# Alternating the transposes of cached keys and of probabilities in a fused decoder layer's attention

## The chip, the cores and the metric

One core of a Trainium2 chip runs the whole program. Its engines work side by side, each through its own list of instructions, and meet at semaphores: TensorE (PE: matmuls and transposes, results to the eight PSUM banks), VectorE (DVE), ScalarE (ACT), GpSimd (POOL), and SyncE (SP), which issues the DMAs. The metric is device microseconds of one execution, lower is better.

## The reference, cut to what matters

One layer step for a prompt of 1024 tokens and for 8 samples of 8 new tokens. The change lies in the first attention of both.

```python
for window, dil in ((128, 1), (512, 4), (2048, 16)):     # 12 heads of 64
    # prompt: every query over strided keys of the prompt
    # sample: 8 queries over strided keys of a cache of 2048 rows and the 8 new rows
    s = einsum(q, k) * 64 ** -0.5 + bias(distance)
    p, lse = softmax(s), logsumexp(s)
    out = p @ v
att = combine(outs, lses)                                # by the softmax denominators
x = x + concat(att, conv) @ w_out                        # then cross attention, SwiGLU, final norm
```

The three branches are folded into one softmax over all keys, by a bias row that holds the branches' weights and masks.

## The kernel before

The attention stage has 24 **steps** `d` for the prompt (6 pairs of heads by 4 pairs of query blocks) and 12 **units** `u` for the samples (two samples, four heads each). Two steps go with one unit: `d = 2u` is the even step, `d = 2u + 1` the odd one. TensorE's list for a step (lines 1207 to 1226) is what the change touches.

- `turn_p(d - 1)`: the probabilities of the step before (tile `sp`, 18 blocks of 128x128) are transposed, four blocks to a PSUM bank, with two blocks of spread reciprocals (`rrec`) behind them. It fills five banks. ScalarE copies each to `p_T` (L1667).
- `turn_keys(u, j)`: cached keys (tile `kb`, loaded by DMA) are transposed, four blocks to a bank. An even step does `j = 0` (four banks) right after `turn_p`, and `j = 1` (four banks) later. An odd step does `j = 2` (two banks). VectorE copies each to `kt01` or `kt2` (L2117).
- `turn_sample_p(u - 1)`, in even steps: the samples' probabilities of the unit before (`srow`) are transposed, three banks. They must have gone through ScalarE's exponential `sample_softmax` (L1678, semaphore `sx_done`).
- `scores(d)`: six matmuls q by k to banks 0 to 3. VectorE adds the bias and takes the maximum (L2126), ScalarE takes the exponential (L1673).
- `sample_scores`, `sample_values`, `values(d - 1)`: the rest of the step's products (L1126, L1131, L1196, L1172).

All transposes and values share the three banks 4, 5 and 6. The table `FILL` numbers the fills of these banks in TensorE's order. Fill `f` goes to bank `4 + f % 3`, and TensorE waits before it (`t_free`) until the fill three before it has been copied out. The copying engines read the same table, so they follow any order of it.

ScalarE's list for an even step (L1690 on) is: the five copies of `turned_p(d - 1)`, then `sample_softmax(u - 1)`, then `turned_sample_p(u - 1)`, then `softmax(d)`. VectorE's is: in every eighth step first `new_rows` (L2110, 16 small copies of bias rows), the key copies, the bias and maximum of the scores, and so on. The diff changes neither list but for the banks named in it.

SyncE reloads a key buffer when its last bank has been transposed (`keys_turned`, L714). There are two buffers, so `j = 2` of one unit and `j = 1` of the next share one.

Of the kernel before, what the change touches and what calls it, by code (L numbers as in the profile page):

```python
# [26 lines left out]
P = 128  # L27
# [54 lines left out]
def layer_step(nc, A):  # L82

    ctx = ExitStack()
    with ctx:
        def sem(name):
            return ctx.enter_context(nc.semaphore(name))
# [257 lines left out]
        kn_in = [sem(f"kn_in{i}") for i in range(2)]  # L345
# [142 lines left out]
        FILL = {}  # L488

        def number(kind, at, count):  # L490
            for i in range(count):
                FILL[kind, at, i] = len(FILL)

        for d in range(STEPS):
            u, second = divmod(d, 2)
            if d:
                number("P", d - 1, 5)
            if second:
                number("K2", u, 2)
                if u:  # L500
                    number("OS", u - 1, 1)
                number("O", d - 1, 1)
                if u:
                    number("OT", u - 1, 1)
            else:
                number("K0", u, 4)
                if u:
                    number("PS", u - 1, 3)
                number("K1", u, 4)
                if d:  # L510
                    number("O", d - 1, 1)
# [6 lines left out]
        KEY_DMAS = (6, 6, 2)  # L518
# [6 lines left out]
        def member_columns(g):  # L525
            return slice(P * (g // 2), P * (g // 2) + P)
# [39 lines left out]
        def _(sp_):  # L566
# [248 lines left out]
            def part_done(kind, n, i=0):  # L815
                _, b, turn = xfill(kind, n, i)
                sp_.wait_ge(xf_full[b], turn + 1)
# [155 lines left out]
        def _(pe):  # L973
# [116 lines left out]
            def fill(kind, at, i=0):  # L1090

                f = FILL[kind, at, i]
                if f >= 3:
                    pe.wait_ge(t_free[f % 3], f // 3)
                return bank[4 + f % 3], t_full[f % 3]
# [4 lines left out]
                    f = FILL[kind, at, i]  # L1100
                    pe.wait_ge(t_free[f % 3], f // 3 + 1)

            def turn_keys(u, j):

                q = 3 * u + j
                turns = q // 2 + 1
                pe.wait_ge(kn_in[q % 2], 16 * sum(KEY_DMAS[p % 3] for p in range(q % 2, q + 1, 2)))
                for i in range(2 if j == 2 else 4):
                    out, full = fill(f"K{j}", u, i)
                    for k in range(4):  # L1110
                        g, t = (i, k) if j < 2 else (2 * i + k // 2, k % 2)
                        last = pe.transpose(out[:, k * P:(k + 1) * P], kb[q % 2][:, g % 2, t, member_columns(g)],  # L1112
                                            ident[:, :])
                    last.then_inc(full, 1)

            def sample_scores(u, j):

                emptied(f"K{j}", u, 2 if j == 2 else 4)
                if 3 * u + j:
                    pe.wait_ge(sr_done, 3 * u + j)  # L1120
                else:
                    pe.wait_ge(kv_done, 36)
                for g in range(4):
                    c, b = member(u, g)
                    keys = kt2[:, g, :] if j == 2 else kt01[:, g, :]
                    last = pe.matmul(bank[7][32 * g:32 * g + 32, 0:256 if j == 2 else 512], q_blk[:, c, b, :], keys,  # L1126
                                     start=True, stop=True)
                if j == 2:
                    for g in (0, 2):
                        c, b = member(u, g)  # L1130
                        last = pe.matmul(bank[7][32 * g:32 * g + 64, 256:256 + TS],  # L1131
                                         q_blk[:, c, b:b + 2, :].rearrange("p b r -> p (b r)"),
                                         k_T[c][:, TP:T], start=True, stop=True)
                last.then_inc(st_ready, 1)

            def scores(d):

                c = d // 4
                for m, (h, _, _, n, key0, qb, at) in enumerate(chunks(d)):
                    if m >= 4:  # L1140
                        pe.wait_ge(sc_free, 6 * d + m - 3)
                    elif d:
                        pe.wait_ge(sc_free, 6 * (d - 1) + (m + 5 if m < 2 else m + 1))
                    half = slice(HD * h, HD * h + HD)
                    pe.matmul(bank[at][:, 0:n], q_T[c][half, qb * P:(qb + 1) * P], k_T[c][half, key0:key0 + n],
                              start=True, stop=True).then_inc(sc_ready, 1)

            def turn_p(d):

                for i in range(5):  # L1150
                    pe.wait_ge(ex_done, 4 * d + (3 if i < 2 else 4))
                    out, full = fill("P", d, i)
                    for k in range(4 * i, min(18, 4 * i + 4)):
                        h, at = divmod(k, 9)
                        last = pe.transpose(out[:, (k - 4 * i) * P:(k - 4 * i + 1) * P], sp[:, h, at * P:(at + 1) * P],
                                            ident[:, :])
                    if i == 4:
                        pe.wait_ge(rr_spread, 4 * d + 4)
                        for s in range(2):
                            last = pe.transpose(out[:, (2 + s) * P:(3 + s) * P], rrec[:, s, :], ident[:, :])  # L1160
                    last.then_inc(full, 1)

            def values(d):

                c, a = divmod(d, 4)
                emptied("P", d, 5)
                out, full = fill("O", d)
                for s, qb in enumerate((a, 7 - a)):
                    for k in range(qb + 1):
                        for h in range(2):  # L1170
                            at = 9 * h + (a + 1) * s + k
                            last = pe.matmul(out[HD * h:HD * h + HD, s * P:(s + 1) * P],  # L1172
                                             v_nat[c][:, k, HD * h:HD * h + HD], p_T[:, at * P:(at + 1) * P],
                                             start=k == 0, stop=k == qb)
                last.then_inc(full, 1)

            def turn_sample_p(u):

                pe.wait_ge(sx_done, u + 1)
                for i, (t0, t1) in enumerate(NEW_TILES):  # L1180
                    out, full = fill("PS", u, i)
                    for t in range(t0, t1):
                        n = P if t < KT else TS
                        last = pe.transpose(out[0:n, (t - t0) * P:(t - t0 + 1) * P], srow[:, t * P:t * P + n], ident[:, :])
                    last.then_inc(full, 1)

            def sample_values(u):

                emptied("PS", u, 3)
                pe.wait_ge(vn_in, 16 * VALUE_DMAS * (u + 1))  # L1190
                out, full = fill("OS", u)
                for t in range(KT + 1):
                    for g in range(4):
                        c = member(u, g)[0]
                        keys = vn[:, g % 2, t, member_columns(g)] if t < KT else vs_nat[:, c * P:(c + 1) * P]
                        last = pe.matmul(out[32 * g:32 * g + 32, 0:P], pT_s[:, t, 32 * g:32 * g + 32], keys,  # L1196
                                         start=t == 0, stop=t == KT)
                last.then_inc(full, 1)

            def turn_sample_out(u):  # L1200
                emptied("OS", u, 1)
                out, full = fill("OT", u)
                pe.transpose(out[:, 0:P], o_sb[:, :], ident[:, :]).then_inc(full, 1)
# [2 lines left out]
            pe.wait_ge(kv_done, 6 * PAIRS)  # L1206
            for d in range(STEPS):
                u, second = divmod(d, 2)
                if d:
                    turn_p(d - 1)  # L1210
                turn_keys(u, 2 if second else 0)
                if u and not second:
                    turn_sample_p(u - 1)
                scores(d)
                if second:
                    sample_scores(u, 1)
                    if u:
                        sample_values(u - 1)
                    sample_scores(u, 2)
                else:  # L1220
                    sample_scores(u, 0)
                    turn_keys(u, 1)
                if d:
                    values(d - 1)
                if second and u:
                    turn_sample_out(u - 1)
# [230 lines left out]
            for v in range(XU + 3):  # L1457
# [8 lines left out]
                if 2 <= v < XU + 2:  # L1466
                    u = v - 2
# [7 lines left out]
                if v >= 3 and (v - 3) % 4 == 3:  # L1475
                    u = v - 3
# [1126 lines left out]
```

## Time and profile before

| | |
|---|---|
| median of 3 runs | 2029.76 us (2029.33 to 2029.76) |
| profiled execution | 2030.58 us |
| its span in the trace | 2028.8 us |
| TensorE busy over the span | 94% |
| granted TensorE clock, mean | 0.983 |
| attention stage (first to last key transposes) | 327.9 to 657.0 us |

Times in the rows are us from the span's start. "Idle before" is the time that an engine waited ahead of a group of instructions, and after the arrow stands what ended the wait. Matmuls overlap each other, so a group's first start and the next group's first start tell more than the durations.

### The profile page before, as it was taken

How to read it: one execution, taken by the hardware profiler on the slowest of the kernel's cores; microseconds unless marked ns; L12 is line 12 of the kernel's file. 1: busy time of each engine (PE TensorE's matmuls, PEld its weight loads, DVE VectorE, ACT ScalarE, POOL GpSimd, SP SyncE). 2: the span in 40 equal slices, each digit the busy share in tenths (PEclk: the TensorE clock that was granted, in tenths of full speed). 3: DMA queues.
4: the chain of work that ended last, by engine and by line, in shares of the span. 5: the costliest groups of instructions: out<-in, count | busy, mean ns of one | idle time of the engine just before them, and what ended most of it. 6: DMA issues, size and time to landing. Idle time of an engine off the chain costs nothing. (4 is left out here: it accounts for less than half of the span.)

```text
span 2028.8 us, 33274 instructions
## 1 busy us (share of the span) xinstructions
PE 1906.5 (94%) x13253; PEld 1764.3 (87%) x13253; DVE 1049.0 (52%) x2108; ACT 440.4 (22%) x902; POOL 508.5 (25%) x377
## 2 busy tenths in 40 slices
PE   6999996999999899899989999999999999999987
PEld 6999995666666799899648989999999999999987
DVE  6698635676666453512543354544544544544455
ACT  5000022555455421200431131001001001000005
POOL 2333221010100134452002223233332233333220
PEclk9999998999999999999999989999999999999998
DMA  4499958698888612124530123432433342311102
GB/s 150 141 339 339 311 177 205 158 212 212 212 208 220 182 42 73 52 84 147 175 105 21 47 70 132 166 124 83 165 124 113 144 161 86 124 42 47 46 21 89
DMA packets 221891, 281.38 MB, mean 139 GB/s; under 512 B 9409, under 2 KB 208457, under 8 KB 220041
## 3 DMA queue, kind: packets, MB, share of 16 engines
q1 hardware_dynamic: 221789, 279.95, 45.5%
q8 instruction: 72, 1.18, 0.2%
q14 instruction: 30, 0.25, 0.0%
HBM read 266.48 MB, written 113.89 MB: 187 GB/s over the span
## 5 line engine op out<-in xcount | busy, mean ns | idle before, releaser
L908 POOL CAST w_hi<-w_raw 128x1024 fp32r<-128x1024 f32 x98 | 105.3, 1075 | 980.2 <-issue 332.8
L1526 PE MATMUL bank<-g_lo,w_hi 128*128 128x362 f32 (+1 forms) x1056 | 350.4, 332 | 0.0
L1526 PE MATMUL bank<-g_hi,w_lo 128*128 128x362 f32 (+1 forms) x1056 | 350.3, 332 | 0.0
L1526 PE MATMUL bank<-g_hi,w_hi 128*128 128x362 f32 (+1 forms) x1056 | 347.8, 329 | 2.2 <-DVE g_lo L2454 2.2
L910 POOL TENSOR_TENSOR w_lo<-w_raw,w_hi 128x1024 fp32r<-128x1024 f32 x98 | 265.3, 2707 | 7.8
L1526 PEld LDWEIGHTS bank<-g_hi,w_hi 128*128 128x128 f32 x1056 | 199.7, 189 | 2.6 <-DVE g_lo L2454 2.5
L1526 PEld LDWEIGHTS bank<-g_hi,w_lo 128*128 128x128 f32 x1056 | 201.0, 190 | 0.0
L2531 DVE TENSOR_TENSOR xT<-bank,xT 128x362 f32<-128x362 f32 (+1 forms) x264 | 139.8, 534 | 116.2 <-PE bank L1546 116.2
L1526 PEld LDWEIGHTS bank<-g_lo,w_hi 128*128 128x128 f32 x1056 | 199.5, 189 | 0.0
L1546 PE MATMUL bank<-act_hi,w_hi 128*128 128x364 f32 (+1 forms) x528 | 176.3, 334 | 16.3 <-DVE xT L2531 10.2
L1546 PE MATMUL bank<-act_lo,w_hi 128*128 128x364 f32 (+1 forms) x528 | 174.2, 330 | 0.0
L1546 PE MATMUL bank<-act_hi,w_lo 128*128 128x364 f32 (+1 forms) x528 | 174.2, 330 | 0.0
L1054 PE MATMUL bank<-h_hi,w_hi 128*128 128x362 f32 (+1 forms) x432 | 146.1, 338 | 5.3 <-POOL w_lo L910 5.3
L1054 PE MATMUL bank<-h_hi,w_lo 128*128 128x362 f32 (+1 forms) x432 | 142.5, 330 | 0.0
L1054 PE MATMUL bank<-h_lo,w_hi 128*128 128x362 f32 (+1 forms) x432 | 142.3, 329 | 0.0
L1289 PE MATMUL bank<-g_hi,w_hi 128*128 128x362 f32 (+1 forms) x384 | 127.7, 333 | 3.5 <-DVE g_lo L2225 2.8
L1289 PE MATMUL bank<-g_lo,w_hi 128*128 128x362 f32 (+1 forms) x384 | 129.8, 338 | 0.0
L1289 PE MATMUL bank<-g_hi,w_lo 128*128 128x362 f32 (+1 forms) x384 | 127.5, 332 | 0.0
L1546 PEld LDWEIGHTS bank<-act_hi,w_hi 128*128 128x128 f32 x528 | 100.2, 190 | 21.4 <-DVE xT L2531 15.1
L2482 DVE TENSOR_TENSOR f_in<-bank,factor 128x362 f32<-128x362 f32 (+1 forms) x66 | 35.1, 534 | 145.9 <-PE bank L1526 145.7
L2487 DVE SCALAR_TENSOR_TENSOR gated<-gated,bank 128x362 f32<-128x362 f32 (+1 forms) x66 | 34.9, 528 | 143.2 <-PE bank L1526 143.2
L2117 DVE COPY kt<-bank 128x512 f32<-128x512 f32 x120 | 75.4, 683 | 64.6 <-PE bank L1112 64.5
(289 smaller groups left out, 3651.3 us busy)
## 6 DMA issues: line engine op xcount, KB each, us to landing
out_sk_dram<-in_cache_win_k_dram SPq DMA_DIRECT2D x24, 2040.0 KB
out_sv_dram<-in_cache_win_v_dram SPq DMA_DIRECT2D x24, 2040.0 KB
vn<-in_cache_win_v_dram SPq DMA_DIRECT2D x24, 576.0 KB, 7.4
kb<-in_cache_win_k_dram SPq DMA_DIRECT2D x48, 256.0 KB, 5.4
vn<-in_cache_win_v_dram SPq DMA_DIRECT2D x24, 512.0 KB, 8.9
w_raw<-in_w_in_dram SPq DMA_DIRECT2D x22, 512.0 KB, 10.2
w_raw<-in_w_ffn_gate_dram SPq DMA_DIRECT2D x22, 512.0 KB, 3.8
w_raw<-in_w_ffn_up_dram SPq DMA_DIRECT2D x22, 512.0 KB, 3.8
```

The costliest lines, as they stand in the source:

```text
L908: pool.tensor_copy(w_hi[slot][:, :], w_raw[slot][:, :]).then_inc(w_hi_done, 1)
L910: pool.tensor_tensor(w_lo[slot][:, :], w_raw[slot][:, :], w_hi[slot][:, :].bitcast(F32), ALU.subtract).then_inc(w_ready[slot], 1)
L1054: last = pe.matmul(out, w, r, start=start, stop=stop)
L1289: last = pe.matmul(out, w, r, start=start, stop=stop)
L1526: last = pe.matmul(out, w, r, start=start, stop=stop)
L1546: last = pe.matmul(bank[6 + r % 2][:, 0:w], wt[slot][:, j * 512 + o * P:j * 512 + (o + 1) * P], rhs[:, j, t0:t0 + w], start=j == 0 and m == 0,
L2117: dve.tensor_copy(dst, src[:, :]).then_inc(free, 1)
L2482: dve.tensor_tensor(f_in[:, t0:t0 + w], bank[g][:, 0:w], factor[:, t0:t0 + w], ALU.mult).then_inc(f_gate, 1)
L2487: dve.scalar_tensor_tensor(out=out, in0=out, scalar=0.5, in1=bank[3 + g][:, 0:w], op0=ALU.mult, op1=ALU.mult).then_inc(f_gated, 1)
L2531: dve.tensor_tensor(place, bank[6 + r % 2][:, 0:w], place, ALU.add).then_inc(d_added, 1)
```

## The change

In a step, TensorE now goes through the fills P0, key 0, P1, key 1 and so on, until the keys of that place (four banks in an even step, two in an odd one) run out, and then through the rest of P. `FILL` is numbered so too. The wait for the keys' DMA stands before the first key fill, which is now the second fill of the step and was the sixth.

```diff
+        def first_keys(d):
+            return ("K2", 2) if d % 2 else ("K0", 4)
+
         for d in range(STEPS):
             u, second = divmod(d, 2)
-            if d:
-                number("P", d - 1, 5)
+            kind, count = first_keys(d)
+            for i in range(5):
+                if d:
+                    FILL["P", d - 1, i] = len(FILL)
+                if i < count:
+                    FILL[kind, u, i] = len(FILL)
             if second:
-                number("K2", u, 2)
...
             else:
-                number("K0", u, 4)
...
-            def turn_keys(u, j):
+            def turn_keys(u, j, fills):
                 q = 3 * u + j
-                turns = q // 2 + 1
-                pe.wait_ge(kn_in[q % 2], 16 * sum(KEY_DMAS[p % 3] for p in range(q % 2, q + 1, 2)))
-                for i in range(2 if j == 2 else 4):
+                if 0 in fills:
+                    pe.wait_ge(kn_in[q % 2], 16 * sum(KEY_DMAS[p % 3] for p in range(q % 2, q + 1, 2)))
+                for i in fills:
...
-            def turn_p(d):
-                for i in range(5):
+            def turn_p(d, fills=range(5)):
+                for i in fills:
...
             for d in range(STEPS):
                 u, second = divmod(d, 2)
-                if d:
-                    turn_p(d - 1)
-                turn_keys(u, 2 if second else 0)
+                for i in range(5):
+                    if d:
+                        turn_p(d - 1, [i])
+                    if i < first_keys(d)[1]:
+                        turn_keys(u, 2 if second else 0, [i])
                 if u and not second:
                     turn_sample_p(u - 1)
                 scores(d)
...
-                    turn_keys(u, 1)
+                    turn_keys(u, 1, range(4))
```

TensorE in even step 6, before: `sp` and `rrec` are the probabilities with their reciprocals, `kb1` the keys, `srow` the samples' probabilities.

```order
L1155 MATMUL bank5<-ident,sp 128x128 x4
L1155 MATMUL bank6<-ident,sp 128x128 x4
L1155 MATMUL bank4<-ident,sp 128x128 x4
L1155 MATMUL bank5<-ident,sp 128x128 x4
L1155 MATMUL bank6<-ident,sp 128x128 x2
L1160 MATMUL bank6<-ident,rrec 128x128 x2
L1112 MATMUL bank4<-ident,kb1 128x128 x4
L1112 MATMUL bank5<-ident,kb1 128x128 x4
L1112 MATMUL bank6<-ident,kb1 128x128 x4
L1112 MATMUL bank4<-ident,kb1 128x128 x4
L1184 MATMUL bank5<-ident,srow 128x128 x4
```

The same place of the changed kernel (L1161 is the transpose of `sp`, L1118 that of the keys, L1190 that of `srow`):

```order
L1161 MATMUL bank5<-ident,sp 128x128 x4
L1118 MATMUL bank6<-ident,kb1 128x128 x4
L1161 MATMUL bank4<-ident,sp 128x128 x4
L1118 MATMUL bank5<-ident,kb1 128x128 x4
L1161 MATMUL bank6<-ident,sp 128x128 x4
L1118 MATMUL bank4<-ident,kb1 128x128 x4
L1161 MATMUL bank5<-ident,sp 128x128 x4
L1118 MATMUL bank6<-ident,kb1 128x128 x4
L1161 MATMUL bank4<-ident,sp 128x128 x2
L1166 MATMUL bank4<-ident,rrec 128x128 x2
L1190 MATMUL bank5<-ident,srow 128x128 x4
```

The last fill of the probabilities, with `rrec`, was the fifth of nine and is the ninth. The third fill of the probabilities goes to the bank that the first keys were in (bank 6), and waits until VectorE has copied them.

TensorE in odd step 7, before, from the first fill to the first score (L1145):

```order
L1155 MATMUL bank4<-ident,sp 128x128 x4
L1155 MATMUL bank5<-ident,sp 128x128 x4
L1155 MATMUL bank6<-ident,sp 128x128 x4
L1155 MATMUL bank4<-ident,sp 128x128 x4
L1155 MATMUL bank5<-ident,sp 128x128 x2
L1160 MATMUL bank5<-ident,rrec 128x128 x2
L1112 MATMUL bank6<-ident,kb1 128x128 x4
L1112 MATMUL bank4<-ident,kb1 128x128 x4
L1145 MATMUL bank0<-k_T1,xT 128x512
```

The same place of the changed kernel (L1151 is the score):

```order
L1161 MATMUL bank4<-ident,sp 128x128 x4
L1118 MATMUL bank5<-ident,kb1 128x128 x4
L1161 MATMUL bank6<-ident,sp 128x128 x4
L1118 MATMUL bank4<-ident,kb1 128x128 x4
L1161 MATMUL bank5<-ident,sp 128x128 x4
L1161 MATMUL bank6<-ident,sp 128x128 x4
L1161 MATMUL bank4<-ident,sp 128x128 x2
L1166 MATMUL bank4<-ident,rrec 128x128 x2
L1151 MATMUL bank0<-k_T1,xT 128x512
```

The two key fills moved from places six and seven to two and four, and what follows the seven fills is unchanged.

## Rows read from the trace of the kernel before

**Rows 1.** The page: busy us, share of the span and instructions of each engine.

```profile
PE 1906.5 (94%) x13253; PEld 1764.3 (87%) x13253; DVE 1049.0 (52%) x2108; ACT 440.4 (22%) x902; POOL 508.5 (25%) x377
```

**Rows 2.** Windows, step 2 to the end of the stage: busy, clock, DMA share, GB/s.

```profile
358.60:677.00 318.40, 299.04 (x3413) 219.05 (x3411) 202.91 (x785) 167.51 (x363) 21.73 (x99) 0.99 0.85 204
```

**Rows 3.** Waits, 320 to 690 us: who waited for whom, total, times, longest.

```profile
PE bank L1112 <- DMA kb<-in_cache_win_k_dram: 17.8, 6, 8.8
PEld bank L1184 <- ACT srow L1678: 6.6, 11, 2.4
```

**Rows 4.** Timeline, TensorE, even step 6: start, duration, instructions.

```profile
413.33 2.40 PE L1155 MATMUL bank<-ident,sp 128*128 128x128 f32 x18
415.57 0.38 PE L1160 MATMUL bank<-ident,rrec 128*128 128x128 f32 x2
415.82 2.07 PE L1112 MATMUL bank<-ident,kb 128*128 128x128 f32 x16
418.09 1.48 PE L1184 MATMUL bank<-ident,srow 128*128 128x128 f32 x11 [0.21 <-ACT srow L1678]
```

**Rows 5.** Timeline, ScalarE and VectorE, even step 6.

```profile
413.97 2.68 ACT L1667 ACTIVATE p_T<-bank 128x512 f32<-128x512 f32 x5 [3.43 <-PE bank L1155]
416.48 2.48 DVE L2117 COPY kt<-bank 128x512 f32<-128x512 f32 x4 [2.41 <-PE bank L1112]
416.51 1.44 ACT L1678 ACTIVATE srow<-srow,snm 128x1344 f32<-128x1344 f32 x1
```

**Rows 6.** Timeline, TensorE, the stage's last transposes and what follows.

```profile
668.79 0.38 PE L1160 MATMUL bank<-ident,rrec 128*128 128x128 f32 x2
671.30 1.42 PE L1184 MATMUL bank<-ident,srow 128*128 128x128 f32 x11 [2.13 <-ACT srow L1678]
672.74 3.85 PE L1172 MATMUL bank<-p_T,v_nat 128*64 128x128 f32 x36
454.81 2.19 PE L1172 MATMUL bank<-p_T,v_nat 128*64 128x128 f32 x36
```

**Rows 7.** Timeline, TensorE and VectorE, step 8, then step 16.

```profile
441.09 2.40 PE L1155 MATMUL bank<-ident,sp 128*128 128x128 f32 x18
441.86 3.51 DVE L2110 COPY d_new<-d_strip 32x8 f32<-32x8 f32 x16
445.40 2.49 DVE L2117 COPY kt<-bank 128x512 f32<-128x512 f32 x4
446.14 0.66 PE L1112 MATMUL bank<-ident,kb 128*128 128x128 f32 x4 [1.02 <-DVE kt L2117]
446.83 1.65 PE L1184 MATMUL bank<-ident,srow 128*128 128x128 f32 x11
554.95 2.40 PE L1155 MATMUL bank<-ident,sp 128*128 128x128 f32 x18
558.54 2.48 DVE L2117 COPY kt<-bank 128x512 f32<-128x512 f32 x4
559.98 1.65 PE L1184 MATMUL bank<-ident,srow 128*128 128x128 f32 x11
```

**Rows 8.** Timeline, TensorE, odd step 7.

```profile
428.33 2.33 PE L1155 MATMUL bank<-ident,sp 128*128 128x128 f32 x18
431.74 2.40 PE L1145 MATMUL bank<-k_T,xT 64*128 64x512 f32 x10
```

**Rows 9.** Timeline, TensorE, step 9, and the keys' arrival in step 1.

```profile
460.69 1.09 PE L1112 MATMUL bank<-ident,kb 128*128 128x128 f32 x8 [1.21 <-DMA kb<-in_cache_win_k_dram]
347.56 1.97 PE L1112 MATMUL bank<-ident,kb 128*128 128x128 f32 x8 [6.77 <-DMA kb<-in_cache_win_k_dram]
349.45 3.44 PE L1145 MATMUL bank<-k_T,xT 64*128 64x256 f32 x12
```

**Rows 10.** Windows, after the waits of rows 9 and rows 6: the clock stands third from the end.

```profile
345.20:351.90 6.70, 4.34 (x16) 3.25 (x18) 2.47 (x8) 0.53 (x3) 0.00 (x0) 0.50 1.05 268
672.90:676.20 3.30, 3.30 (x34) 3.30 (x34) 0.00 (x0) 0.60 (x3) 0.00 (x0) 0.50 1.08 317
```

## The prediction, made before the changed kernel ran

> **What bounds the kernel now.** I read the page first. TensorE is busy for 94% of the span [rows 1], so over the whole program time is lost where TensorE waits or runs slowly. The change touches one stage, so I read that stage by windows: from step 2 to the end of the stage TensorE is busy 299 of 318 us at a clock of 0.99, while the DMA share is 0.85 and VectorE and ScalarE are busy for 203 and 168 us [rows 2]. TensorE is the pace there, with two engines close behind it that must each answer in time. The list of waits shows what TensorE waits for: DMA of the keys, 17.8 us in six waits with one of 8.8 at the start of the stage, and, each time it comes to the samples' probabilities, ScalarE's exponential `srow`, 6.6 us in 11 waits on the weight loads [rows 3]. The second is small but regular: it says that in an even step two paths end at the same place, TensorE's transposes and ScalarE's copies plus exponential. The timeline of an even step shows both.
>
> **The even step, path by path.** In step 6 the first transpose of `sp` starts at 413.33, the keys at 415.82 and the samples' probabilities (line 1184) at 418.09 [rows 4]. So five fills of probabilities take 2.49 us and the samples come 4.76 us after the start. ScalarE starts its five copies at 413.97 and the exponential at 416.51, for 1.44 us [rows 5]; TensorE has waited 0.21 us for it although four key fills lie between [rows 4]. The path is: last fill of `sp` and `rrec`, its copy, exponential, first transpose of `srow`. It takes 418.09 - 415.82 = 2.27 us from the end of that last fill. The end of the stage shows the same path without keys in between: the `rrec` transposes start at 668.79, two of them are over by 669.0, and `srow` starts at 671.30, 2.3 us later, of which TensorE is idle for 2.13 [rows 6]. So today four key fills cover this path almost exactly.
>
> The change puts these four key fills ahead of the last fill of probabilities, and nothing takes their place behind it: the ScalarE list is unchanged, with the exponential behind all five copies. A transpose goes by in 0.11 to 0.12 us where nothing stalls (twelve in 1.55 us with a tail of 0.27 would be 0.116; 16 keys in rows 4 give the same). The nine fills hold 18 + 2 + 16 = 36 transposes, 4.0 to 4.15 us. Then comes the path of 2.27, so the samples start at 6.3 to 6.4 us after the step's start, not at 4.76. I take +1.5 us for an ordinary even step, since the stalls of the probabilities' run (2.49 against 20 x 0.113 = 2.26) should go. Bounds: +1.3, if ScalarE answers faster without a queue of its own copies, to +1.8, the whole time of four fills. Behind the waiting transposes of `srow` stand `scores(d)`, and VectorE and ScalarE wait for those, so nothing fills the hole and all that follows comes later by as much. Nine even steps (2, 4, 6, 10, 12, 14, 18, 20, 22): 9 x 1.5 = **+13.5 us**.
>
> **Steps 8 and 16.** Here VectorE first makes 16 small copies (line 2110), and copies the first keys only at 445.40, that is 4.31 us after the step's start at 441.09 [rows 7]. Before, only the ninth fill needed that bank: it starts at 446.14, at 5.05, and the samples at 446.83, at 5.74. In the new order the bank of the first keys is wanted by the third fill of probabilities, the fifth of nine. It can't start before 5.05 either, and five fills follow from there (20 transposes, 2.25 us), then the path of 2.27: 9.57, which is +3.8. Step 16 by the same sum: start 554.95, key copies 558.54, so bank free at 3.59 + 0.74 = 4.33, then 4.52 more, 8.85 against 559.98 - 554.95 = 5.03 [rows 7], again +3.8. Together **+7.6 us** (bounds 6 to 9).
>
> **Odd steps.** No exponential stands in the way here; scores follow the seven fills. In step 7 they start 431.74 - 428.33 = 3.41 us after the first fill [rows 8]. 28 transposes are 3.16 us, so alternating engines may save 0.2. For the seven odd steps that don't wait for DMA (3, 5, 7, 11, 13, 15, 19): **-1.4 us** (0 to -2.5).
>
> The key wait, too, moves from the sixth fill to the second. In the odd steps 9, 17, 21 and 23 the keys arrive later than TensorE wants them. What was done before the wait (four fills of `sp`) now comes behind it. But each of these steps comes after an even step that is itself later by 1.5 or 3.8, while the loads depend on events of the steps before. So the wait neither grows nor is paid twice. In step 9 the wait is 1.21 us [rows 9], and step 8 gives 3.8 us more time for the load: I take -1.1 there and -0.5 in step 17. Steps 21 and 23 I take at nothing. Together **-1.6 us** (-3 to +3).
>
> Step 1 has no such step ahead. Its keys land at 347.56 after 6.77 us of waiting, and the eight transposes behind take 349.45 - 347.56 = 1.89 us [rows 9], at a clock of 0.50 that lasts to 351.9 [rows 10]. Now 24 transposes stand behind the wait. At half clock throughout they cost 24 x 0.236 = 5.7 us, at full clock 2.7, so the step loses 0.8 to 3.8 us. With the clock up again at 351.9 it would be 3.1; the scores then run faster, so I take **+2.8 us**.
>
> **The clock.** The idle time of 2.13 us at the stage's end is followed by a clock of 0.50 from 672.9 to 676.2 [rows 6, 10]: 1.2 GHz in place of 2.4. The values there take 3.85 us where they take 2.19 at full clock [rows 6], so one such fall costs up to 1.7. Waits of 1.02 and 1.21 us in steps 8 and 9 [rows 7, 9] were followed by no fall: rows 2 show 0.99 over all of it. The 11 new idle times are like the first of these, but one case is no rule: none may be followed by a fall, or all 11 (0 to +19 us). Part of a slow stretch would lie over scores, which VectorE paces anyway, so I price one at 1.0 and count six: **+6 us**. The Trainium skill, page "TensorE: Matmul & The Clock Gate", section "Part 1: The HAM clock gate", says that the throttled state is the default and activity releases it, so idle time on TensorE is not free beyond its own length. The trace agrees at 672.9. By that rule alone I would put this term in its upper half.
>
> **The sum.** 13.5 + 7.6 - 1.4 - 1.6 + 2.8 + 6 = +26.9 us. The profiled execution took 2030.58 (span 2028.8 and 1.8 around it), which gives 2057.5. The median of the runs is 0.8 lower than that execution, so the forecast is **2057 us**. Without falls of the clock it would be 2051.
>
> **The rivals.**
>
> *Faster, because two engines empty the banks in turn.* Before, ScalarE has five fills in a row at about 0.5 us each (2.68 us for five [rows 5]) and VectorE four at 0.6 (2.48), while TensorE fills at 0.45. Alternating gives each engine 0.9 us per bank. If nothing else held the step up, the samples would follow the nine fills at 4.1 us and not at 4.76: 11 x 0.6 and 12 x 0.2 are 9 us, hence about 2021 us. For this to come out, the exponential must not be late, which rows 3 speak against: it is already the last to arrive in 11 of 11. This case is the one that the skill favours: "PSUM — Partial Sum Buffer", section "Specifications (TRN2)", has ScalarE and VectorE read PSUM side by side at full bandwidth as long as they are in different banks. By it the stalls would go, a gain in the range just given. Chance 0.05.
>
> *No change, because DMA sets the pace.* The DMA share is 0.85 [rows 2]. If landings alone set when steps go on, idle time of TensorE would only replace waiting for keys. But of the 17.8 us [rows 3], 8.8 lie at the stage's start and 6.77 in step 1 [rows 9], so 2.2 us are left after it, and there is hardly anything to replace. The key buffers come free one to three fills earlier, which can give back that much and no more. Time if it held: 2030. Chance 0.04.
>
> *Slower than forecast, with a fall of the clock in every even step.* 20.9 + 11 x 1.7 = 39.6, hence about 2069. For: the tail's two rows. Against: half of such a stretch covers scores. Chance 0.10. The remaining 0.81 is the forecast.
>
> **Range and chances.** All terms at their low ends (11.7 + 6 - 2.5 - 3 + 0.8, no falls) give +13, 2043; all at their high ends with falls in every step give +51, 2081. Neither is likely at once. The forecast's own spread is 2045 to 2065; to leave out no more than 2 in 10 with the harder case, the range is 2045 to 2067. A measurement of this kernel can tell some 0.2%, 4 us. Faster by more than that 0.04 (most of the first rival), within it 0.05, slower 0.91.
>
> **What would show it.** In step 6 of the new trace the samples' transposes should start 6.1 to 6.5 us after the first fill, with TensorE idle about 2.1 us before them, released by ScalarE's `srow`; in the list of waits this line should grow from some 7 to about 24 us. In steps 8 and 16 TensorE should stop after four fills until VectorE's first key copy is done. Odd steps should reach their scores after 3.2 us. Windows of the stage should show a clock under 0.99. I am wrong if the exponential starts before the last copy of probabilities, if the wait for `srow` stays near 0.2 us, or if the stage is not some 20 us longer.

## The result, and the profile after

| | before | after |
|---|---|---|
| median | 2029.76 us (5 runs, 2029.33 to 2033.91) | 2066.25 us (5 runs, 2063.92 to 2072.25) |
| profiled execution, span | 2028.8 us | 2070.4 us |
| granted clock, mean | 0.983 | 0.973 |

The changed kernel is slower: ratio 1.0184, 95% interval 1.0165 to 1.0203, some 37 us. The forecast was 27 us more.

The waits of TensorE in the stage (320 to 735 us; total, times, longest):

```profile
PE bank L1190 <- ACT srow L1686: 25.0, 12, 2.1
PE bank L1118 <- DMA kb<-in_cache_win_k_dram: 18.3, 3, 8.9
PE bank L1178 <- issue: 4.2, 2, 3.0
PE bank L1161 <- DVE kt L2125: 3.8, 2, 2.4
```

The wait for the exponential `srow`, of which rows 3 showed a trace, is now the longest in total. Even step 6 on TensorE, to be read beside [rows 4] (start, duration, count):

```profile
423.75 0.60 PE L1161 MATMUL bank<-ident,sp 128*128 128x128 f32 x4
424.34 0.63 PE L1118 MATMUL bank<-ident,kb 128*128 128x128 f32 x4
424.81 0.60 PE L1161 MATMUL bank<-ident,sp 128*128 128x128 f32 x4
425.24 0.60 PE L1118 MATMUL bank<-ident,kb 128*128 128x128 f32 x4
425.84 0.63 PE L1161 MATMUL bank<-ident,sp 128*128 128x128 f32 x4
426.31 0.60 PE L1118 MATMUL bank<-ident,kb 128*128 128x128 f32 x4
426.74 0.60 PE L1161 MATMUL bank<-ident,sp 128*128 128x128 f32 x4
427.18 0.63 PE L1118 MATMUL bank<-ident,kb 128*128 128x128 f32 x4
427.78 0.41 PE L1161 MATMUL bank<-ident,sp 128*128 128x128 f32 x2
428.03 0.38 PE L1166 MATMUL bank<-ident,rrec 128*128 128x128 f32 x2
430.49 2.02 PE L1190 MATMUL bank<-ident,srow 128*128 128x128 f32 x11 [2.08 <-ACT srow L1686]
```

VectorE's first key copy there, and ScalarE, beside [rows 5]: the copy of the fifth fill, that of the ninth, and the exponential:

```profile
425.01 0.69 DVE L2125 COPY kt<-bank 128x512 f32<-128x512 f32 x1 [0.51 <-PE bank L1118]
...
426.51 0.60 ACT L1675 ACTIVATE p_T<-bank 128x512 f32<-128x512 f32 x1 [0.47 <-PE bank L1161]
...
428.44 0.60 ACT L1675 ACTIVATE p_T<-bank 128x512 f32<-128x512 f32 x1 [0.46 <-PE bank L1166]
428.94 1.41 ACT L1686 ACTIVATE srow<-srow,snm 128x1344 f32<-128x1344 f32 x1
430.24 0.19 ACT L1686 ACTIVATION_READ_ACCUMULATOR srow<-srow,snm 128x1 f32 x1
```

The samples' transposes start 430.49 - 423.75 = 6.74 us after the step's first fill (4.76 before). The exponential stands behind the last copy, as it did, and nothing covers it: 2.2 us from the last fill's end to the samples. The stage's clock fell, beside [rows 2] with 0.99:

```profile
363.70:722.00 358.30, 311.27 (x3417) 229.79 (x3418) 209.69 (x789) 176.96 (x369) 21.80 (x99) 0.95 0.77 184
```

In step 8 TensorE stops after four fills, until VectorE's first key copy is done, and the samples start 468.94 - 459.94 = 9.00 us after the step's first fill:

```profile
459.94 1.06 PE L1161 MATMUL bank<-ident,sp 128*128 128x128 f32 x4
...
464.29 0.63 PE L1161 MATMUL bank<-ident,sp 128*128 128x128 f32 x4 [1.49 <-DVE kt L2125]
...
468.94 1.33 PE L1190 MATMUL bank<-ident,srow 128*128 128x128 f32 x5 [2.08 <-ACT srow L1686]
```

One place was not foreseen. In step 7 TensorE stops in the middle of `values`, for nothing that the profile names:

```profile
452.55 0.49 PE L1178 MATMUL bank<-p_T,v_nat 128*64 128x128 f32 x5
456.07 3.68 PE L1178 MATMUL bank<-p_T,v_nat 128*64 128x128 f32 x31 [3.02 <-issue]
```

The rest of the values then run at a clock of 0.50 (456.1 to 459.9).

### The profile page after: what moved, and what is told of

Read it like the earlier page. It is cut to its first block and busy times, and to the rows that moved or that the text cites. A ratio compares the mean times of both kernels' runs of the same rounds, so it can differ in the third digit from the quotient of the medians.

```text
span 2070.4 us, 33274 instructions
## 1 busy us (share of the span) xinstructions
PE 1918.7 (93%) x13253; PEld 1774.5 (86%) x13253; DVE 1055.9 (51%) x2108; ACT 448.1 (22%) x902; POOL 506.3 (24%) x377
## 5 line engine op out<-in xcount | busy, mean ns | idle before, releaser
L1876 ACT ACTIVATE f_th<-f_in 128x362 f32<-128x362 f32 (+1 forms) x66 | 33.4, 508 | 341.7 <-DVE f_in L2490 341.7
```

The costliest lines, as they stand in the source:

```text
L1876: act.activation(f_th[:, t0:t0 + w], f_in[:, t0:t0 + w], ACT.Tanh, scale=0.5)\
```

## Experiments

Theory 1: the loss is the samples' exponential, which waits for the last fill of probabilities, now later by four key fills; idle time, and falls of the clock behind it. Theory 2: alternating itself is slow, by the banks' round trips. Theory 3: the keys' DMA is wanted four fills earlier. Each median stands against runs of the kernel before on the same chip; those ran from 2023 to 2039 us, so ratios are used, with a 95% interval in brackets. An account by steps is that of one profiled execution.

**r1: the changed kernel again.** 

> The changed kernel once more, as the partner of the runs below. Both theories expect 2064 to 2068 us. The new question is the two places of its first profile that the order of fills does not explain: 3.0 us of idle time in step 7 that is put down to issue, and a start of step 1 that is 2 us later. If they are chance, this profile lacks at least the first, and its span is 2062 to 2066.

Measured: 2066.78 us against 2031.67, ratio 1.0183 (1.0161 to 1.0205). The stop in step 7 is there again, at the same matmul, so it is not chance alone. It took 3.02 us in the first profile:

```profile
453.53 3.68 PE L1178 MATMUL bank<-p_T,v_nat 128*64 128x128 f32 x31 [4.01 <-issue]
```

This profile (span 2065.0) lies at the median, so it is the one for an account. Growth of a step is how much later the next step's first fill starts than in the profile of before, less the same for its own first fill:

```
steps                            growth, us          sum
2 4 12 18 20 (even, clock whole) 1.87 to 1.93        9.6
6 10 14 22   (even, a fall)      2.9 3.6 2.9 3.05   12.4
8 16         (late key copies)   4.6 5.2             9.7
0 1          (first keys)        1.3 2.2             3.5
7            (the stop)          6.2                 6.2
9 17 21      (waits for keys)    -1.5 -0.5 -0.5     -2.4
15           (a shorter stop)    -0.4               -0.4
3 5 11 13 19 (other odd)         -0.1 to 0.0        -0.1
23 (-0.7) and after the stage (-1.5)                -2.2
total = 2065.0 - 2028.8                             36.2
```

"A fall" is a step in which the granted clock went to 0.50. (The rows add up to 36.3 by rounding.) Of step 0's 1.3 us, 1.26 is a later start of the stage's first key transposes. That start moves from one profile to the next whatever the order of fills (0.9 to 4.7 us later in the other eleven than in the profile of before), so it is not shown to be the change's.

**r2: alternating in odd steps alone**, and **r3: in even steps alone.**

```diff
+            return alternate if d % 2 else in_a_row        # r2
+            return in_a_row if d % 2 else alternate        # r3
```

> Alternating in odd steps alone, even steps as before. Theory 1 (the samples' exponential stands behind the last copy of probabilities, and the keys now go ahead of it): nothing of the loss is left but step 1, +1 to +3 us against before, 2030 to 2033. Theory 2 (alternating itself costs, since every fill waits for a bank's round trip): the odd steps keep their share, some 0.5 to 1 us each, 2036 to 2042. Theory 3 (keys' DMA is wanted earlier): waits for keys in odd steps grow, 2035 or more.

> Alternating in even steps alone, odd steps as before. Theory 1: nearly all of the loss stays, 2061 to 2066, and samples' transposes start 6.7 us after an ordinary even step's start. Theory 2: about half of it, 2048. Theory 3: the loss goes mostly, 2035 to 2040, since the tight loads are those of odd steps.

Measured: r2 2036.68 us, ratio 1.0037 (1.0017 to 1.0057); r3 2067.50, ratio 1.0175 (1.0154 to 1.0196). Nearly all the loss is in the even steps: r3 keeps it. That speaks against theory 3 as the main cause (2035 to 2040 expected of r3), and against theory 2 in the odd steps. Whether the banks' round trips cost much in the even steps is left to r5. r2 is above theory 1's figure and inside those of the other two, and its 12 executions spread from 2028 to 2048 us; the profile, at 2032.69, is one of the fast ones. In it the odd steps that wait for no keys keep their pace (growth -0.1 to 0.0), so theory 2 has no share there. Of its steps after the first two only 9 and 17 grow, by 3.9 and 2.0 us; in step 23 the wait for keys goes from 0.65 to 2.7. In step 9 TensorE waits at the second fill:

```profile
460.80 0.66 PE L1167 MATMUL bank<-ident,sp 128*128 128x128 f32 x4
465.19 0.66 PE L1124 MATMUL bank<-ident,kb 128*128 128x128 f32 x4 [3.74 <-DMA kb<-in_cache_win_k_dram]
```

So theory 3 has a share where no longer even step gives the load more time. In r3 the step-7 stop is absent, yet the total is the same. Step 8 grows by 8.2 us there, 3.7 more than in r1: TensorE waits 3.03 us for VectorE's first key copy (1.38 in r1), and the clock stands at 0.50 from 455.3 to 468.8 (in r10, after the same wait, at 1.00 to 463.8). Six of the nine ordinary even steps have a fall of the clock, against r1's four.

**r4: the kernel before, with the exponential ahead of the copies.**

```diff
                 u, second = divmod(d, 2)
+                if u and not second:
+                    sample_softmax(u - 1)
                 if d:
                     turned_p(d - 1)
                 if u and not second:
-                    sample_softmax(u - 1)
                     turned_sample_p(u - 1)
                 softmax(d)
+            sample_softmax(UNITS - 1)
             turned_p(STEPS - 1)
-            sample_softmax(UNITS - 1)
             turned_sample_p(UNITS - 1)
```

> The kernel before, with the samples' exponential moved ahead of the five copies of probabilities on ScalarE, at the end of the stage too. Theory 1: the samples' transposes no longer wait, and start 4.4 us after an even step's start in place of 4.76; 11 x 0.35 and 2.1 at the end are 6 us, 2024. Rival: the exponential holds up the copies by its 1.6 us, TensorE then waits for banks and nothing is won, 2030, or 11 x 1 us are lost, 2041.

Measured: 2033.62 us, ratio 1.0008 (0.9995 to 1.0021): no gain, a miss. Step 4 shows that the exponential does lie in ScalarE's idle time ahead of the step, and that the copies are not held up:

```profile
389.84 1.42 ACT L1678 ACTIVATE srow<-srow,snm 128x1344 f32<-128x1344 f32 x1 [2.04 <-DVE snm L2166]
391.50 2.68 ACT L1667 ACTIVATE p_T<-bank 128x512 f32<-128x512 f32 x5
...
390.86 2.40 PE L1155 MATMUL bank<-ident,sp 128*128 128x128 f32 x18
395.44 1.65 PE L1184 MATMUL bank<-ident,srow 128*128 128x128 f32 x11
397.02 0.92 PE L1145 MATMUL bank<-k_T,xT 64*128 64x128 f32 x6
```

The samples start at 4.58 us, but the scores at 6.16, as in step 6 of the kernel before (419.50 - 413.33 = 6.17):

```profile
419.50 0.59 PE L1145 MATMUL bank<-k_T,xT 64*128 64x384 f32 x2
```

VectorE's four key copies end 5.6 us after the step's start in both kernels (at 396.48 here, at 418.96 there [rows 5]), and the samples' last fill, which takes the bank of the fourth, starts 0.06 us later in both. Two paths ended together; taking one away shows the other. At the stage's end the 2.1 us are won, and the wait for `vn` after it grows from 2.3 to 5.8 us.

**r5: the changed kernel with the same edit.** 

> The changed kernel with the samples' exponential moved ahead of the copies of probabilities on ScalarE. Theory 1 (the late exponential is the loss): TensorE does not stop before the samples' transposes in ordinary even steps, they start at 4.6 to 4.7 us, and no fall of the clock follows. Left are steps 8 and 16 (third fill of probabilities waits for VectorE, 1.5 us each) and the earlier key wait in steps 1, 9 and 17 (1.8 to 3.8 each): 2036 to 2042. Theory 2 (alternating itself is the loss): 2050 or more.

Measured: 2041.09 us against 2031.29, ratio 1.0051 (1.0032 to 1.0070). Nearly three quarters of the loss are gone by an edit on ScalarE alone, TensorE's order untouched. The same edit without the new order won nothing (r4), so it acts on what the order brought. This is the main proof of theory 1. Step 6:

```profile
417.15 0.60 PE L1161 MATMUL bank<-ident,sp 128*128 128x128 f32 x4
...
421.43 0.38 PE L1166 MATMUL bank<-ident,rrec 128*128 128x128 f32 x2
421.65 1.40 PE L1190 MATMUL bank<-ident,srow 128*128 128x128 f32 x11
422.98 0.59 PE L1151 MATMUL bank<-k_T,xT 64*128 64x384 f32 x2
```

The samples follow the nine fills at once, at 4.50 us, and scores start at 5.83. An ordinary even step grows by -0.34 to -0.40, so the nine banks' round trips cost nothing on balance, and theory 2 falls for the even steps too. What is left are steps 0 and 1 (2.8 and 1.9), 8 (0.75), 16 (3.0), the stop of step 7 (5.1) and a wait for keys in step 23 (3.9); behind the stage 5.0 us are given back. The profile is of an execution of 2037.62, 3.5 under the median.

**r6: two key fills ahead of the last fill of probabilities, not four.**

```diff
+            return [(0, 0), (1, 0), (0, 1), (1, 1), (0, 2), (0, 3), (0, 4), (1, 2), (1, 3)]
```

> The changed kernel, but in even steps only two of the four key fills go ahead of the last fill of probabilities (P K P K P P P K K), and ScalarE's order as it was. Theory 1: a dose. The samples' transposes start at 5.6 to 5.8 us (4.76 with none ahead, 6.74 with four); idle time before them is 1.3 us and, since waits of 1.0 to 1.4 were followed by no fall of the clock, no falls: +14 to +17, 2045 to 2049. Theory 2: loss goes by the number of alternations, five in place of eight, 2053.

Measured: 2048.07 us, ratio 1.0091 (1.0068 to 1.0113). Step 6:

```profile
418.38 0.60 PE L1168 MATMUL bank<-ident,sp 128*128 128x128 f32 x4
...
424.15 1.42 PE L1197 MATMUL bank<-ident,srow 128*128 128x128 f32 x11 [1.23 <-ACT srow L1693]
```

Start at 5.77, and each ordinary even step grows by 0.90 to 0.96: half the dose, half the growth, and no fall of the clock in an ordinary even step. The time is inside theory 1's range, below theory 2's figure.

**r7: useless transposes in the idle time.**

```diff
                 if u and not second:
+                    pe.wait_ge(sr_done, 3 * u)
+                    for _ in range(16):
+                        pe.transpose(bank[7][:, 0:P], ident[:, :], ident[:, :])
                     turn_sample_p(u - 1)
```

> The changed kernel with 16 transposes of the identity into bank 7 (whose contents have been read by then) just before the samples' transposes of each even step: work of no use that keeps TensorE going for 1.8 of its 2.2 idle us. The samples' transposes still start at 6.7 us. If falls of the clock make up a third of the loss, they go and the time is 2056 to 2060. If the falls cost nothing beyond the idle time (scores are paced by VectorE), 2065 to 2067.

Measured: 2056.89 us, ratio 1.0129 (1.0103 to 1.0156), with 176 transposes more than the changed kernel, and by the ratios 11 us less. Step 6, and the stage's window (r1's, then r7's):

```profile
419.30 0.60 PE L1161 MATMUL bank<-ident,sp 128*128 128x128 f32 x4
...
423.79 1.91 PE L1223 MATMUL bank<-ident 128*128 128x128 f32 x16
426.04 1.42 PE L1190 MATMUL bank<-ident,srow 128*128 128x128 f32 x11 [0.34 <-ACT srow L1689]
```

```profile
361.00:717.00 356.00, 307.95 (x3437) 227.21 (x3437) 211.85 (x799) 177.70 (x373) 22.32 (x102) 0.96 0.78 185
```

```profile
360.80:711.00 350.20, 324.30 (x3687) 246.19 (x3684) 213.64 (x798) 179.68 (x379) 21.75 (x99) 0.98 0.80 194
```

The samples start at 6.74 us as before, and all nine ordinary even steps grow by 1.87 to 1.93. In r1 four of them grew by 1.0 to 1.6 more, 4.7 us in all: the price of the falls there. The stop in step 7 (6.2 in r1) is absent in r7, so against r1 two things differ. r10 below lacks the stop too, but has falls in seven of the nine steps: these grow by 26.1 us in r10 and by 17.3 in r7, and the ratios, 1.0176 and 1.0129 with intervals that don't overlap, are 9.5 us apart.

**r8: exponential first, alternating only in even steps other than 8 and 16.** 

> Exponential first, alternating in even steps other than 8 and 16 alone, odd steps in a row. By theory 1 this has none of the losses and what alternating saves: the scores of an ordinary even step start at 5.9 to 6.1 us in place of 6.16, 1 to 2 us in all, 2029 to 2032, which can't be told from the kernel before. Theory 2: 9 even steps keep their share, 2040 or more.

Measured: 2028.97 us against 2031.29, ratio 0.9991 (0.9978 to 1.0004). The interval takes in 1, so it does not beat the kernel before for certain. In step 6 the scores start at 5.82 us, and all nine alternating steps grow by -0.34 to -0.39, -3.1 us in all. Against that stands step 1, which starts 4.9 us later in its profile; that figure is 1.3 to 4.9 over the profiles here, whatever the kernel.

**r9: steps 8 and 16 in the old order.**

```diff
+            return alternate if d % 8 else in_a_row
```

> The changed kernel with steps 8 and 16 (and 0, which is the same either way) in the old order. Prices their term: in its second profile they lose 4.6 and 5.2 us, and steps 9 and 17 give 1.5 and 0.5 back. Theory 1 expects 7 to 8 us less than the changed kernel, 2058 to 2061. If what is lost there is only moved on to the next waits for DMA, 2064 to 2067.

Measured: 2062.25 us against 2028.66, ratio 1.0164 (1.0145 to 1.0183). Growth of steps 8 and 16 goes to -0.7 and +0.3, 10.1 us less than in r1, but steps 17 and 12 grow by 1.7 and 1.6 more, six ordinary even steps have a fall of the clock in place of four, and the ratio differs from r1's by 0.0019, some 4 us, with intervals that overlap. Between the two expectations: part of the loss there is moved on.

**r10: 16 useless transposes in step 2 alone.** 

> The changed kernel with 16 transposes of the identity in step 2 alone, which move the rest of TensorE's list on by 16 transposes and, lying in idle time, should cost nothing. Both profiles of the changed kernel stop for 3.0 and 4.0 us at the same instruction of values in step 7, while the profile names no other engine. If the stop belongs to that place in the list (as a fetch of instructions would), it goes or moves, and up to 6 us with it: 2060 to 2063. If it belongs to what happens in step 7, it stays: 2065 to 2067.

Measured: 2065.09 us, ratio 1.0176 (1.0158 to 1.0194). The stop is gone; step 7's values run through:

```profile
450.97 2.14 PE L1178 MATMUL bank<-p_T,v_nat 128*64 128x128 f32 x36
```

Its growth is 0.03 us in place of 6.2. That alone does not tie the stop to a place in the list, for no stop comes at the old place either (number 2827 of TensorE's matmuls, now a matmul of the sample scores). A smaller stop does it. In step 15 all twelve profiles have one of 0.8 to 1.8 us in `values`, put down to issue: in eleven at matmul 4055, the profile of before included. In r10 it is still at 4055, which is now 16 matmuls earlier in the step's work. So that stop hangs on the place in TensorE's list, not on the work. The place is not the same in every list, though: in r7, with 112 matmuls put in ahead, the stop is at 4183, 128 further on.

The total hardly shows that step 7 is free of its stop. Step 8 waits 3.05 us for VectorE in place of 1.38 and grows by 0.8 more; seven of the nine ordinary even steps grow by 2.9 to 3.5 us in this profile, each with a fall, where r1 has four falls, and steps 0 and 1 grow by 1.7 us more.

## Why the prediction was right in kind and short in size

The path named was the right one, and it was named with its place: last copy, exponential, samples' transposes, 2.2 us without cover. r5 removes it and r6 halves it. The sum was 26.9 us, the profile of r1 has 36.2: 9.3 us short. The terms, against r1:

| term | forecast | measured |
|---|---|---|
| nine ordinary even steps | 13.5 | 17.3 (9 x 1.92) |
| falls of the clock | 6 | 4.7 in these steps, more in 8 and 16 |
| steps 8 and 16 | 7.6 | 9.7, falls included |
| odd steps, pace | -1.4 | -0.1 |
| odd steps, waits for keys | -1.6 | -2.4 |
| steps 0 and 1 | 2.8 (step 1) | 3.5 (step 1: 2.2) |
| the stop in step 7 | none | 6.2 |
| step 15; step 23 and after the stage | none | -0.4, -2.2 |

**The step that failed in size** is the length of the nine fills in the even steps' term: 36 transposes in "4.0 to 4.15 us". They take 4.50 (r5, where the samples follow at once). With the path of 2.24 us behind them the samples start at 6.74, not at 6.3 to 6.4, and the term is 17.3 us, not 13.5. I took the extra time of the probabilities' run (2.49 us against 2.26) for stalls by a slow ScalarE, which alternating would remove. But some 0.15 us of it is a stop at the second fill, which is there in both orders: 424.34 - 423.75 = 0.59 where a fill takes 0.44, and 0.59 too in step 6 of the kernel before. And alternating adds two more of this size, at the fifth and the ninth fill (425.84 - 425.24 and 427.78 - 427.18 are 0.60). Both of these wait for a bank that VectorE emptied: its first keys' fill starts at 424.34, the copy runs from 425.01 to 425.70, and the bank is filled again at 425.84, a round trip of 1.50 us, while three fills of 0.44 are 1.32. The round trip through ScalarE is shorter: fill at 425.84, copy from 426.51 to 427.11, fill again at 427.18, 1.34 us, and TensorE hardly stops there. By the single records the nine fills took 4.39 us before and 4.49 alternating. For the same reason odd steps saved nothing: scores at 3.43 us in place of 3.41, where -1.4 us had been put down.

With it falls the faster rival. Even where the exponential is out of the way (r5), the even step gains 0.34 us and not 0.6. The copies take 0.60 and 0.69 us each while they overlap, as they did in turn, so neither engine's own rate got worse; the one bank's round trip was the limit. That agrees with the Trainium skill ("PSUM — Partial Sum Buffer", section "Specifications (TRN2)": both engines read PSUM at full bandwidth from different banks), but nothing follows from it for the time.

**Falls of the clock** were priced at 1.0 and counted six. r1 has six in the eleven steps, four of them in ordinary ones at 1.0 to 1.6 each; the first profile has six in ordinary ones, 8.0 us in all, and r10 seven, 8.8. The count differs between runs of almost the same list, so a single profile can't settle it. That r1's count came out as forecast is luck. In r7, where the idle time is filled, they are gone from all nine.

**Steps 8 and 16** behaved as said: the fifth fill waits for VectorE's first key copy (2.35 to 2.5 us in step 16). The samples' start moved from 5.74 to 8.99 and from 5.03 to 9.20; the forecast was 9.57 and 8.85. Without the stop ahead of it, step 8 comes to 9.79 (r10).

**DMA** was right in the changed kernel: the wait of step 9 went. The claim rested on the longer even step, and r2, where that is missing, shows the price otherwise, 3.9 and 2.0 us.

**What I did not have** is the stop in step 7: 6.2 us, a sixth of r1's loss and two thirds of what the sum was short by. It is not a fixed price, though. r3 and r10 don't have it and are as slow (1.0175, 1.0176), with more falls of the clock and a longer step 8 in its place. So the fills' part of the shortfall is shown, 3.8 us in even and 1.3 in odd steps; how the rest is shared out between the stop and the falls differs from one execution to the next. The profile of before has a short stop of the kind (line 1172, put down to issue, 1.41 us at 553.5), and I read past it.

## What to carry to other kernels

Before work is moved ahead of an instruction, ask who waits for that instruction on another engine, and what covers that path now. Here four fills did, to within 0.2 us. Then ask for the second path that ends at the same place: r4 removed the first and won nothing. Where a few buffers rotate, compare the round trip of one buffer with the time of the fills between. Here the second engine did not shorten it: its round trip was 1.50 us against 1.34.

## What the runs showed that I had not expected

- TensorE stopped for 3.0 to 4.0 us at the same matmul of step 7 in five profiles (the changed kernel twice, r5, r6, r9), with no engine named. Before, r2, r3, r4 and r8 have the matmul at the same place in the list and don't stop, so place and timing both count. The traces point at instructions that arrive late. Beside the data's 280 MB they hold an instruction queue (q8) with transfers of 16 KB. All five stops, and the twelve of step 15, end 1.2 to 1.7 us after the end of such a transfer (r1: transfer from 450.73 to 451.91, TensorE goes on at 453.53). In the five profiles that have the matmul of step 7 in its place without a stop, the last transfer ended 2.9 to 4.7 us ahead of it. No run moved a transfer by itself, and why it starts later in some kernels stays open.
- Idle times of 2.1 us were followed by a fall of the granted clock to 0.50 (1.2 GHz) in four (r1) to seven (r10) of nine ordinary even steps, six in the first profile; r6's, of 1.2 us, in none.
- Useless transposes in an idle stretch left the kernel faster, not slower: ratio 1.0129 against 1.0183 without them. With them no ordinary even step had a fall of the clock.
